# The lower halves of the gate one-hots made on ScalarE, two steps ahead, and ten row slots moved to the spreading units

## The chip, the cores and the metric

The kernel runs on one core of one Trainium2 chip. The metric is the device time of one execution in microseconds (us), lower is better. The engines are TensorE (PE in the rows, its weight loads PEld), VectorE (DVE), ScalarE (ACT), GpSimd (POOL) and SyncE (SP).

## What is computed

One layer of an encoder trunk over 1,024 tokens of width 1,024, in float32. The first half of the layer (gated mixing and a short convolution) is not touched by the change. The second half is PEER, a product-key mixture of 16,384 single-neuron experts:

```python
def block(xb):                       # 128 tokens
    q = (xb @ w_q).reshape(t, PEER_HEADS, 2, PEER_HALF)
    s = jnp.einsum('thpd,hpkd->thpk', q, sub_keys)
    s1, i1 = lax.top_k(s[:, :, 0], PEER_TOPK)
    s2, i2 = lax.top_k(s[:, :, 1], PEER_TOPK)
    ...
    top_s, sel = lax.top_k(cand_s, PEER_TOPK)
    idx = jnp.take_along_axis(cand_i, sel, axis=-1)
    gate = jax.nn.softmax(top_s, axis=-1)
    u = jnp.take(expert_u, idx, axis=0)
    act = jax.nn.gelu(jnp.einsum('thkd,td->thk', u, xb))
    v = jnp.take(expert_v, idx, axis=0)
    return jnp.einsum('thk,thkd->td', gate * act, v)
```

Each token has 8 heads times 16 chosen experts, 128 (expert, gate) pairs.

## The kernel before

The tokens are in two parts. Part A (3 blocks of 128 tokens) fetches only the experts that it chose: for each of 384 *slots* an indirect DMA on GpSimd's queue gathers one u row per token (128 rows of 4 KB), VectorE forms the dot product (`u_row`, L1016), and later a v row is gathered and added with its weight (`v_row`, L1025). Part B (5 blocks, 640 tokens) computes all 16,384 experts densely on TensorE: 64 units of kind E multiply the tokens by all expert u vectors and store the activations (`a_dram`), and 32 groups of two W units multiply coefficients by all expert v vectors. The coefficient is activation times gate, so the gates must be spread into a dense matrix (`g_dram`). That is done in 20 E units, numbers 40 to 59 (`E_SPREAD` = 40, `N_SPREAD` = 20), the *spreading units*. Everything runs concurrently; the row slots of part A are divided by hand among the units and groups of part B (`_sections`, L179 to L194): so many slots beside each unit.

Each expert table unit arrives as float32 in `stage`; ScalarE makes its upper float16 half (`make_hi`), VectorE the lower (`make_lo`, L913), and TensorE multiplies hi*hi, hi*lo and lo*hi (L1566 to L1568).

**The spreading.** A step q (8 in each spreading unit, 160 in all) covers 4 tokens. VectorE makes one-hots of both key halves, 1,024 float16 elements (`onehot_keys`, L1352), and multiplies the second key's one-hot by the upper and by the lower float16 half of the gates in one operation of 1,024 elements (`onehot_gate`, L1359, `oh_gate[:, q % 4, c]` with c = 0 for upper and 1 for lower). TensorE multiplies them in 8 matmuls of 128 columns into a psX bank (L1697), placed behind the third and the seventh of the eight chunks of each of the unit's four output tiles. ScalarE copies psX into `gbuf` (`spread_out`, L827). The one-hot buffers are a ring of 4 steps: `onehot_keys(q)` waits until TensorE has done step q - 4.

**ScalarE's order in a spreading unit** is, four times, two `spread_out` copies and the evacuation of one output tile; then, at the end of the unit, `make_hi` of the unit four ahead, the issue of the store to `g_dram` (L859), the issue of the store to `a_dram` (L863), and the small gelu on `dots`. An engine takes its instructions in order, so what is behind these DMA issues waits for them. All of ScalarE's activations stand on line L682 in the rows, a helper's line.

**The W groups.** For each group VectorE multiplies activations by gates (L1470), makes the lower half of the coefficients (L1479), makes two lower halves of weights (L913), adds three shared output tiles (L1490), and does its row slots. TensorE does 10 tiles of 12 matmuls of 512 columns.

`SLOTS` is 384. Slots not given to the units before are divided over 31 W groups: 194 of them before the change, so 6 in most groups and 7 in eight groups (numbers 3, 7, 11, 15, 19, 23, 27 and 30). The u rows run 24 slots (`LAG`) ahead of the v rows.

Of the kernel before, what the change touches and what calls it, by code (L numbers as in the profile page):

```python
# [178 lines left out]
def _sections():  # L179

    k = {("B", "U", u): 0 for u in (1, 2, 3)}
    for u in range(16):
        k["B", "M", u] = 3
    for u in range(4):
        k["B", "O", u] = 1
    for h in range(HEADS):
        k["B", "Q", h] = 2
    for e in range(2 * NGRP):
        k["B", "E", e] = 2 if e < E_SPREAD else 1 + e % 2 if e < E_SPREAD + N_SPREAD else 3
    groups = NGRP - 1  # L190
    left = SLOTS - sum(k.values())
    for g in range(groups):
        k["B", "W", 2 * g] = left * (g + 1) // groups - left * g // groups
    return k  # L194
# [65 lines left out]
def trunk_layer(nc, x, c_row, w_cond, b_col, w_front, ln_g, ln_b, w_spat, b_spat, conv_w,  # L260
                ln1_g, ln1_b, keys_t, u_units, v_units, u_rows, v_rows, ln2_g, ln2_b, out):
    with ExitStack() as ctx:
# [6 lines left out]
        def v3(ap, a):  # L269
            return ap.rearrange("p (a b) -> p a b", a=a)  # L270
# [115 lines left out]
        row_at += [R1[:, 1024 * i:1024 * (i + 1)] for i in range(5)]  # L386
        a_ring = v3(R1[:, :], 4)
        keys_t16 = v3(zone(15300, 640, F16), 2)
        gates16 = v3(zone(15940, 640, F16), 2)
        g_t = zone(16580, 640)  # L390
        iota_k4 = v3(zone(17220, 256, F16), P)
        gbuf = [zone(4096 * i, 4096).rearrange("p (k t) -> p k t", t=32) for i in range(2)]
        oh_keys = zone(8192, 4 * 512, F16).rearrange("p (r c k t) -> p r c k t", r=4, c=2, t=4)
        oh_gate = zone(10240, 4 * 512, F16).rearrange("p (r c k t) -> p r c k t", r=4, c=2, t=4)
# [80 lines left out]
        weight_ready = sem("weight_ready")  # L475
        oh_keys_ready = sem("oh_keys_ready")
        oh_ready = sem("oh_ready")
        prod_ready = sem("prod_ready")
        c_hi_ready = sem("c_hi_ready")
        c_ready = sem("c_ready")  # L480
# [11 lines left out]
        def wait_x(eng, a):  # L492
            eng.wait_ge(x_ready, a + 1)
# [186 lines left out]
        def _(act):  # L680
# [77 lines left out]
            for n, (x, kind, u) in enumerate(UNITS):  # L758
# [20 lines left out]
                elif kind == "U":  # L779
                    if u % 2 == 0:  # L780
                        act.wait_ge(evA_free, EVA[x] + 5 + u // 2)
                        feature(n, evAd[x], ACT.Gelu_apprx_tanh)
                    else:
                        act.wait_ge(evB_free, EVB[x] + 8 + u // 2)
                        feature(n, evB[x], ACT.Gelu_apprx_tanh)
                elif kind == "M":
                    q = u // 4
                    if u % 4 == 0:
                        act.wait_ge(evA_free, EVA[x] + 7 + q)
                        feature(n, evAd[x])  # L790
                    elif u % 4 == 2:
                        act.wait_ge(evC_free, EVC[x] + 4 + q)
                        feature(n, evC[x])
                    else:
                        act.wait_ge(evB_free, EVB[x] + 10 + 2 * q + u % 4 // 2)
                        feature(n, evB[x], ACT.Tanh, 0.5 * DESCALE)
                elif kind == "O" and x == "A":
                    for b in range(SB):
                        evacuate(t + b, xt[x][:, b, u * UC:(u + 1) * UC])
                elif kind == "O":  # L800
                    if u == 0:
                        for b in range(DB):
                            for c in range(4):
                                evacuate(T_O + 4 * b + c, xt[x][:, b, c * UC:(c + 1) * UC])
                            if b:
                                root(R_OB + 2 * (b - 1), slice(SB + b - 1, SB + b))
                                root(R_OB + 2 * (b - 1) + 1, slice(SB + b - 1, SB + b))

                            before = ("B", "O", b - 2) if b >= 2 else ("B", "M", 15)
                            if b != 1:  # L810
                                gelu_dots(SEC_OF[before])
                        root(R_OB + 2 * (DB - 1), slice(NB - 1, NB))
                        root(R_OB + 2 * (DB - 1) + 1, slice(NB - 1, NB))
                        gelu_dots(SEC_OF["B", "O", 3])
                        h_hi_tiles("H2B", 0, 2 * KD)
                elif kind == "Q":
                    if x == "A" and u == 0:
                        act.wait_ge(x1_stored["A"], 16)
                        act.wait_ge(h2_ready, 1)
                    feature(n, rk[x]["qb"][u % 2])  # L820
                elif kind == "E":
                    wait(act, a_stored[u % 4], 16 * (u // 4))
                    if u == 0:
                        act.wait_ge(x1_stored["B"], 16 * DB)
                    slot = v3(a_ring[:, u % 4, :], 2)

                    def spread_out(r):  # L827
                        i = u - E_SPREAD
                        for q in range(2):
                            at = 2 * r + q  # L830
                            a = X_G + 8 * i + at
                            wait_x(act, a)
                            activation(gbuf[i % 2][:, :, 4 * at:4 * at + 4],
                                       psX[a % 4][:, :].rearrange("p (t k) -> p k t", t=4),
                                       ACT.Copy, 1.0 / GS).then_inc(x_free[a % 4], 1)

                    spreading = E_SPREAD <= u < E_SPREAD + N_SPREAD
                    if spreading and u >= E_SPREAD + 2:
                        act.wait_ge(g_stored[u % 2], 16 * ((u - E_SPREAD) // 2))
                    for j in range(2):  # L840
                        for half in range(2):
                            if spreading:
                                spread_out(2 * j + half)
                            evacuate(t + 2 * j + half, slot[:, j, half * HB:(half + 1) * HB], ACT.Gelu_apprx_tanh)
# [52 lines left out]
        def _(dve):  # L897
# [429 lines left out]
            def idx_t():  # L1327
# [10 lines left out]
                for i in range(4):  # L1338
                    a = X_IDX + 5 - i
                    dve.wait_ge(x_free[a % 4], a // 4 + 1)  # L1340
                step(V.tensor_copy(gates16[:, 0, :], g_t))
                settle()
                step(V.tensor_tensor(gates16[:, 1, :], g_t, gates16[:, 0, :], ALU.subtract))
                step(V.tensor_copy(iota_k4, iota_i[:, :].unsqueeze(2).to_broadcast([P, P, 4])))
                settle()

# [7 lines left out]

            def onehot_gate(q):
                dve.wait_ge(oh_keys_ready, q + 1)
                at = gates16[:, :, 4 * q:4 * q + 4].unsqueeze(2).to_broadcast([P, 2, P, 4])
                both = oh_keys[:, q % 4, 1:2, :, :].to_broadcast([P, 2, P, 4])
                V.tensor_tensor(oh_gate[:, q % 4, :, :, :], both, at, ALU.mult).then_inc(oh_ready, 1)  # L1359

            def spreads(unit):

# [193 lines left out]
        def _(pe):  # L1556
# [87 lines left out]
            for n, (x, kind, u) in enumerate(UNITS):  # L1644
# [43 lines left out]
                elif kind == "E" and E_SPREAD <= u < E_SPREAD + N_SPREAD:  # L1688
                    def spread(r, s):
                        if s not in (2, 6):  # L1690
                            return
                        q = 8 * (u - E_SPREAD) + 2 * r + (s == 6)
                        pe.wait_ge(oh_ready, q + 1)
                        ps = x_tile(X_G + q)
                        for t in range(4):
                            for c in range(2):
# [92 lines left out]
```

## Time and profile before

| | |
|---|---|
| time, median of 3 runs | 3223.4 us (3216.7 to 3224.55) |
| the profiled execution | 3218.67 us, of which the span of its instructions 3216.9 us |
| mean granted TensorE clock | 0.962 of full |
| TensorE busy | 2928.1 us, 91% of the span |
| VectorE busy | 2635.7 us, 82% |
| ScalarE busy | 812.4 us, 25% |
| GpSimd busy | 1013.3 us, 31% |
| DMA traffic | 917.49 MB, mean 285 GB/s |

Busy time counts instructions that compute; the issue of a DMA isn't counted, although the engine that issues it can stand still for it. The shares are averages over stages of very different kinds, so they don't tell which engine sets the pace in the stage that is changed.

### The profile page before, as it was taken

Reading aid. Unit: us, or ns where it says so; the run is one execution under the profiler, and the core shown is the slowest. Engines: PE = TensorE matmul, PEld = TensorE weight load, DVE = VectorE, ACT = ScalarE, POOL = GpSimd, SP = SyncE. Lnnn points to the kernel's source line nnn. Section 1 sums busy time; section 2 is a strip of 40 time slices with the busy share of each in tenths; the row PEclk is TensorE's granted clock in tenths of the full one; section 3 lists DMA queues with packets and bytes.
Section 4 is the critical chain, followed back from the end, with each engine's and each line's share of the span. In section 5 each row is a group of like instructions: output and inputs, shape, how many; then the busy total and the mean of one; then the engine's idle time right before and its main releaser. Section 6 shows DMA issues by size and latency. Waiting matters only on the chain.

```text
span 3216.9 us, 46792 instructions
## 1 busy us (share of the span) xinstructions
PE 2928.1 (91%) x19088; PEld 1916.7 (60%) x19088; DVE 2635.7 (82%) x4587; ACT 812.4 (25%) x1191; POOL 1013.3 (31%) x778
## 2 busy tenths in 40 slices
PE   4899979997898679999999899999799999999994
PEld 3556666665676556777777688887444444444442
DVE  6865557996765869999999777777699999999987
ACT  2333322111111322222222233333222222222220
POOL 0000000003553104344434311112366666666630
PEclk9999989998999889999999999999899999999997
DMA  9888534333898247877777788888999999999973
GB/s 357 310 321 321 192 142 158 119 112 145 318 358 304 85 178 251 297 276 277 278 283 264 263 262 262 262 262 280 364 392 414 414 414 414 411 415 413 413 285 124
DMA packets 266230, 917.49 MB, mean 285 GB/s; under 512 B 20464, under 2 KB 102432, under 8 KB 222752
## 3 DMA queue, kind: packets, MB, share of 16 engines
q1 hardware_dynamic: 63968, 427.91, 34.7%
q0 software_dynamic: 110592, 402.70, 33.2%
q10 hardware_dynamic: 91456, 83.89, 8.0%
q8 instruction: 151, 2.47, 0.3%
q14 instruction: 63, 0.52, 0.0%
HBM read 771.79 MB, written 142.63 MB: 284 GB/s over the span
## 4 chain that ended last, share of the span: by engine, by line
PE 59%; DVE 25%; issue 9%; DMA 6%; ACT 1%; SPq 0%; POOL 0%; DVEq 0%
PE psU L1566 17%; PE psU L1568 17%; PE psU L1567 17%; PE psX L1697 5%; DVE acc_sp L1025 3%; DMA R<-in_v_rows,idx_sp 2%; DVE w L913 2%; DVE Z L1470 2%; DVE rows L1016 2%; DVE R L1016 2%; DVE Z L1490 1%; PE psX L1566 1%; PE psX L1567 1%; PE psX L1568 1%; DMA rows<-in_v_rows,idx_sp 1%
## 5 line engine op out<-in xcount | busy, mean ns | idle before, releaser
L1566 PE MATMUL psU<-hB,w 128*128 128x320 f16 x3072 | 924.4, 301 | 31.8 <-ACT R L682 19.8
L1568 PE MATMUL psU<-hB,w 128*128 128x320 f16 x3072 | 921.0, 300 | 0.9 <-issue 0.9
L1567 PE MATMUL psU<-hB,w 128*128 128x320 f16 x3072 | 921.1, 300 | 0.0
L913 DVE SCALAR_TENSOR_TENSOR w<-stage,w 128x2048 f16<-128x2048 f32 x176 | 402.6, 2288 | 172.8 <-ACT w L682 168.5
L682 ACT ACTIVATE w<-stage 128x2048 f16<-128x2048 f32 x176 | 335.4, 1906 | 359.9 <-PE psX L1568 294.9
L675 POOL DMA_INDIRECT rows<-in_v_rows,idx_sp x214 | 284.2, 1328 | 349.4 <-DVE rows L1016 210.2
L1566 PEld LDWEIGHTS psU<-hB,w 128*128 128x128 f16 x3072 | 304.1, 99 | 145.6 <-issue 33.5
L675 POOL DMA_INDIRECT rows<-in_u_rows,idx_sp x204 | 253.9, 1245 | 430.5 <-DVE rows L1016 372.3
L1568 PEld LDWEIGHTS psU<-hB,w 128*128 128x128 f16 x3072 | 301.0, 98 | 119.0 <-issue 0.5
L1567 PEld LDWEIGHTS psU<-hB,w 128*128 128x128 f16 x3072 | 304.1, 99 | 112.9 <-issue 1.1
L1566 PE MATMUL psX<-w,Z 128*128 128x512 f16 x768 | 296.0, 385 | 48.2 <-DVE Z L1490 33.0
L1566 PE MATMUL psU<-w,Z 128*128 128x512 f16 (+1 forms) x768 | 267.1, 348 | 44.3 <-DVE Z L1479 22.3
L1567 PE MATMUL psX<-w,Z 128*128 128x512 f16 x768 | 295.7, 385 | 0.0
L1568 PE MATMUL psX<-w,Z 128*128 128x512 f16 x768 | 295.3, 384 | 0.0
L1025 DVE SCALAR_TENSOR_TENSOR acc_sp<-rows,weight_sp,acc_sp 128x1024 f32<-128x1024 f32 x214 | 269.2, 1286 | 14.8 <-DMA rows<-in_v_rows,idx_sp 8.4
L1567 PE MATMUL psU<-w,Z 128*128 128x512 f16 (+1 forms) x768 | 267.0, 348 | 0.0
L1568 PE MATMUL psU<-w,Z 128*128 128x512 f16 (+1 forms) x768 | 266.7, 347 | 0.0
L1016 DVE SCALAR_TENSOR_TENSOR rows<-rows,h_sp 128x1024 f32<-128x1024 f32 x204 | 243.6, 1218 | 5.3 <-DMA rows<-in_u_rows,idx_sp 3.0
L682 ACT ACTIVATE Z<-psU 128x320 f32<-128x320 f32 (+1 forms) x224 | 99.5, 451 | 551.0 <-PE psU L1568 426.0
L675 POOL DMA_INDIRECT R<-in_v_rows,idx_sp x108 | 174.3, 1614 | 137.3 <-DVE R L1016 87.2
L682 ACT ACTIVATE R<-psU 128x320 f32<-128x320 f32 (+1 forms) x296 | 123.1, 427 | 368.8 <-PE psU L1568 332.1
L1566 PE MATMUL psU<-Z,w 128*128 128x384 f16 (+1 forms) x640 | 206.5, 323 | 2.9 <-ACT Z L682 2.9
(237 smaller groups left out, 4627.8 us busy)
## 6 DMA issues: line engine op xcount, KB each, us to landing
stage<-in_u_units SPq DMA_DIRECT2D x64, 1024.0 KB
stage<-in_v_units SPq DMA_DIRECT2D x64, 1024.0 KB
stage<-in_w_front SPq DMA_DIRECT2D x48, 1024.0 KB
hl_dram<-w SPq DMA_DIRECT2D x48, 1024.0 KB, 5.5
w<-hl_dram SPq DMA_DIRECT2D x48, 1024.0 KB
a_dram<-R ACTq DMA_DIRECT2D x64, 640.0 KB
g_dram<-Z ACTq DMA_DIRECT2D x20, 2048.0 KB, 15.4
Z<-a_dram SPq DMA_DIRECT2D x32, 1280.0 KB, 12.1
```

What stands on the lines that cost most here:

```text
L675: pool.indirect_dma_start(row_at[r], None, u_rows if table == "u" else v_rows, bass.IndirectOffsetOnAxis(ap=idx_sp[:, slot:slot + 1], axis ...
L682: return nc.scalar.activation(dst, src, func, scale=scale)
L913: V.scalar_tensor_tensor(w[:, n % NW, 1, :], stage[:, v % 2, :], WS, w[:, n % NW, 0, :], ALU.mult, ALU.subtract).then_inc(lo_done, 1)
L1016: V.scalar_tensor_tensor(row_at[r], row_at[r], 1.0, h2_sp[:, slot % SB, :], ALU.mult, ALU.mult, accum_out=dots[:, c % 4, j:j + 1]).then_in ...
L1025: V.scalar_tensor_tensor(dst, row_at[r], weight_sp[:, slot:slot + 1], dst, ALU.mult, ALU.add).then_inc(row_used, 1)
L1470: ins = V.scalar_tensor_tensor(a, a, AS, G_t[g % 2][:, :, j, :], ALU.mult, ALU.mult)
L1490: V.tensor_tensor(dst, ps_shared[:, :], dst, ALU.add).then_inc(v_free, 1)
L1566: mm(ps, lhs[0](k), rhs[0](k), start=start and s == 0, stop=False)
L1567: mm(ps, lhs[0](k), rhs[1](k), start=False, stop=False)
L1568: last = mm(ps, lhs[1](k), rhs[0](k), start=False, stop=stop and s == n - 1)
L1697: ins = mm(ps[:, t * P:(t + 1) * P], oh_keys[:, q % 4, 0, :, t], oh_gate[:, q % 4, c, :, t], start=(c == 0), stop=(c == 1))
```

## The change

```diff
@@ _sections
-        k["B", "E", e] = 2 if e < E_SPREAD else 1 + e % 2 if e < E_SPREAD + N_SPREAD else 3
+        k["B", "E", e] = 2 if e < E_SPREAD + N_SPREAD else 3
@@ buffers
-        gates16 = v3(zone(15940, 640, F16), 2)
+        gates16 = zone(15940, 320, F16)
...
+        gate_lo = zone(17476, 640)
@@ scalar, kind E
+                    def gates_lo(q):
+
+                        if q >= 8 * N_SPREAD:
+                            return
+                        act.wait_ge(oh_keys_ready, q + 1)
+                        for i in range(4):
+                            ins = activation(oh_gate[:, q % 4, 1, :, i], oh_keys[:, q % 4, 1, :, i], ACT.Copy,
+                                             gate_lo[:, 4 * q + i:4 * q + i + 1])
+                        ins.then_inc(oh_lo_ready, 1)
+
                     def spread_out(r):
                         i = u - E_SPREAD
                         for q in range(2):
                             at = 2 * r + q
                             a = X_G + 8 * i + at
+                            gates_lo(8 * i + at + 2)
                             wait_x(act, a)
...
+                    if u == E_SPREAD:
+                        gates_lo(0)
+                        gates_lo(1)
@@ vector, onehot_gate
-                at = gates16[:, :, 4 * q:4 * q + 4].unsqueeze(2).to_broadcast([P, 2, P, 4])
-                both = oh_keys[:, q % 4, 1:2, :, :].to_broadcast([P, 2, P, 4])
-                V.tensor_tensor(oh_gate[:, q % 4, :, :, :], both, at, ALU.mult).then_inc(oh_ready, 1)
+                at = gates16[:, 4 * q:4 * q + 4].unsqueeze(1).to_broadcast([P, P, 4])
+                key = oh_keys[:, q % 4, 1, :, :]
+                V.tensor_tensor(oh_gate[:, q % 4, 0, :, :], key, at, ALU.mult).then_inc(oh_ready, 1)
@@ tensor, spread
                         pe.wait_ge(oh_ready, q + 1)
+                        pe.wait_ge(oh_lo_ready, q + 1)
```

VectorE's `onehot_gate` now makes the upper half alone (512 elements). The lower half of step q is made by four ScalarE activations of 128 elements, one for each token, whose scale is a column of `gate_lo` in SBUF; they stand just ahead of the copy of step q - 2. The lower gates stay in float32. TensorE waits for both halves. The twenty spreading units had 1 or 2 row slots in turn (30 in all) and now have 2 each (40), so the W groups have 184 slots in place of 194: 6 in each but groups 0 and 15, which have 5.

On ScalarE, at the boundary from the first spreading unit to the second, before the change. Z<-psX is a `spread_out` copy, R<-psU the evacuation of an output tile, w<-stage `make_hi`, and dots the gelu of the row section:

```order
L682 ACTIVATE R<-psU 128x320 [waits tile_ready]
L682 ACTIVATE w<-stage 128x2048 [waits stage_in0]
L859 DMA g_dram<-Z 128x32x128 [waits x_free1,x_free2,x_free0,x_free3]
L863 DMA a_dram<-R 128x1280 [waits tile_free]
L682 ACTIVATE dots<-dots 128x2 [waits row_used]
L682 ACTIVATE Z<-psX 128x128x4 [waits x_ready,a_stored1]
L682 ACTIVATE Z<-psX 128x128x4 [waits x_ready]
```

The same place after the change, with Z<-Z 128x128 the new activations:

```order
L684 ACTIVATE R<-psU 128x320 [waits tile_ready]
L684 ACTIVATE w<-stage 128x2048 [waits stage_in0]
L875 DMA g_dram<-Z 128x32x128 [waits x_free1,x_free2,x_free0,x_free3]
L879 DMA a_dram<-R 128x1280 [waits tile_free]
L684 ACTIVATE dots<-dots 128x2 [waits row_used]
L684 ACTIVATE Z<-Z 128x128 [waits oh_keys_ready,a_stored1]
L684 ACTIVATE Z<-Z 128x128 x3
L684 ACTIVATE Z<-psX 128x128x4 [waits x_ready]
L684 ACTIVATE Z<-Z 128x128 [waits oh_keys_ready]
L684 ACTIVATE Z<-Z 128x128 x3
L684 ACTIVATE Z<-psX 128x128x4 [waits x_ready]
```

The first four new activations behind the two stores belong to step 2 of the unit that begins there; those of its steps 0 and 1 stand ahead of the stores, in the unit before.

On TensorE, at the end of a spreading unit's work between two steps of the spreading, before and then after:

```order
L1566 MATMUL psU<-hB,w 128x320
L1567 MATMUL psU<-hB,w 128x320
L1568 MATMUL psU<-hB,w 128x320
L1697 MATMUL psX<-Z 128x128 [waits x_free2,oh_ready]
L1697 MATMUL psX<-Z 128x128 x7
```

```order
L1582 MATMUL psU<-hB,w 128x320
L1583 MATMUL psU<-hB,w 128x320
L1584 MATMUL psU<-hB,w 128x320
L1714 MATMUL psX<-Z 128x128 [waits x_free2,oh_lo_ready,oh_ready]
L1714 MATMUL psX<-Z 128x128 x7
```

Nothing moves on TensorE, but each step has one wait more, `oh_lo_ready`, and all that is queued behind it waits too.

## Rows read from the trace of the kernel before

**Rows 1.** Section 4 of the page: shares of the chain that ended last.

```profile
PE 59%; DVE 25%; issue 9%; DMA 6%; ACT 1%; SPq 0%; POOL 0%; DVEq 0%
```

**Rows 2.** Windows: us, busy time of each engine, TensorE clock, DMA share, GB/s.

```profile
1820.60:2230.60 410.00, 410.00 (x3192) 337.28 (x3190) 322.89 (x442) 154.61 (x278) 70.03 (x61) 1.00 0.81 262
2305.60:3070.00 764.40, 741.01 (x3369) 331.51 (x3370) 744.88 (x822) 171.84 (x111) 473.23 (x343) 0.98 1.02 411
3070.00:3160.00 90.00, 89.00 (x413) 40.14 (x411) 63.49 (x60) 16.53 (x11) 16.96 (x13) 1.00 0.65 254
```

**Rows 3.** Timeline of ScalarE at a unit boundary: start, duration, instruction, idle before.

```profile
1983.87 0.60 ACT L682 ACTIVATE Z<-psX 128x512 f32<-128x512 f32 x1 [1.98 <-PE psX L1697]
1984.36 0.43 ACT L682 ACTIVATE R<-psU 128x320 f32<-128x320 f32 x1
1984.57 0.38 ACTq L859 DMA_DIRECT2D g_dram<-Z  x1
1984.68 1.92 ACT L682 ACTIVATE w<-stage 128x2048 f16<-128x2048 f32 x1
1984.99 5.38 ACTq L863 DMA_DIRECT2D a_dram<-R  x1
1990.42 0.20 ACT L682 ACTIVATE dots<-dots 128x1 f32<-128x1 f32 x1 [3.83 <-issue]
1990.53 1.08 ACT L682 ACTIVATE Z<-psX 128x512 f32<-128x512 f32 x2
```

**Rows 4.** Timeline of TensorE's weight loads: step 2 of the same unit.

```profile
1990.30 0.70 PEld L1697 LDWEIGHTS psX<-Z 128*128 128x128 f16 x6
```

**Rows 5.** Groups by line of ScalarE, 1840:2231: busy us, mean ns, idle before.

```profile
L682 ACT ACTIVATE Z<-psX 128x512 f32<-128x512 f32 x153 | 89.7, 599 | 168.9 <-PE psX L1697 165.5 <-issue 3.5
L682 ACT ACTIVATE R<-psU 128x320 f32<-128x320 f32 x76 | 33.1, 435 | 0.0
L682 ACT ACTIVATE dots<-dots 128x2 f32<-128x2 f32 x10 | 2.0, 204 | 39.5 <-issue 39.5
L682 ACT ACTIVATE dots<-dots 128x1 f32<-128x1 f32 x9 | 1.8, 203 | 36.4 <-issue 36.4
```

**Rows 6.** Groups by line of VectorE, 1840:2231.

```profile
L1352 DVE TENSOR_TENSOR Z<-Z 128x1024 f16<-128x1024 f16 x149 | 102.7, 689 | 66.9 <-PE psX L1697 64.4
L1359 DVE TENSOR_TENSOR Z<-Z 128x1024 f16<-128x1024 f16 x149 | 102.7, 689 | 2.9
```

**Rows 7.** Timelines of TensorE and ScalarE at the first spreading unit.

```profile
1820.58 0.94 PEld L1697 LDWEIGHTS psX<-Z 128*128 128x128 f16 x8
1821.83 0.19 ACT L682 ACTIVATE dots<-dots 128x2 f32<-128x2 f32 x1
```

**Rows 8.** Timeline of VectorE: lower coefficients, once in each W group.

```profile
2321.60 2.81 DVE L1479 TENSOR_TENSOR Z<-Z 128x2560 f16<-128x2560 f32 x1
...
2484.90 2.81 DVE L1479 TENSOR_TENSOR Z<-Z 128x2560 f16<-128x2560 f32 x1
...
2511.69 2.81 DVE L1479 TENSOR_TENSOR Z<-Z 128x2560 f16<-128x2560 f32 x1
...
2540.68 2.81 DVE L1479 TENSOR_TENSOR Z<-Z 128x2560 f16<-128x2560 f32 x1
...
2567.18 2.81 DVE L1479 TENSOR_TENSOR Z<-Z 128x2560 f16<-128x2560 f32 x1
...
3081.95 2.81 DVE L1479 TENSOR_TENSOR Z<-Z 128x2560 f16<-128x2560 f32 x1
```

**Rows 9.** Timeline of TensorE in the W groups, behind a short and a long wait.

```profile
2397.22 0.38 PE L1566 MATMUL psX<-w,Z 128*128 128x512 f16 x1 [1.16 <-DVE Z L1490]
...
2398.95 0.38 PE L1568 MATMUL psX<-w,Z 128*128 128x512 f16 x1
...
2426.28 0.59 PE L1566 MATMUL psX<-w,Z 128*128 128x512 f16 x1 [3.00 <-issue]
...
2429.65 0.38 PE L1568 MATMUL psX<-w,Z 128*128 128x512 f16 x1
```

More of the change, by code:

```diff
@@ L477, in trunk_layer @@
         oh_ready = sem("oh_ready")
+        oh_lo_ready = sem("oh_lo_ready")
         prod_ready = sem("prod_ready")
@@ L1340, in idx_t @@
                     dve.wait_ge(x_free[a % 4], a // 4 + 1)
-                step(V.tensor_copy(gates16[:, 0, :], g_t))
+                step(V.tensor_copy(gates16, g_t))
                 settle()
-                step(V.tensor_tensor(gates16[:, 1, :], g_t, gates16[:, 0, :], ALU.subtract))
+                step(V.tensor_tensor(gate_lo, g_t, gates16, ALU.subtract))
                 step(V.tensor_copy(iota_k4, iota_i[:, :].unsqueeze(2).to_broadcast([P, P, 4])))
```

## The prediction

> **What bounds the kernel now.** I read the chain that ended last first: 59% of the span is TensorE and 25% VectorE [rows 1], so the pace changes hands between stages, and each stage must be read by itself. The windows do that [rows 2]. In the 20 spreading units (1820.6 to 2230.6 us) TensorE is busy for all of the 410 us at full clock; a unit takes 410 / 20 = 20.5 us, a step of the spreading 2.57 us. VectorE has 87 us to spare there and ScalarE seems to have 255. In the W groups (2305.6 to 3070) VectorE is busy for 745 of 764 us and TensorE waits 23. DMA is at 1.02 of its engines and 411 GB/s, so it is about as full as VectorE. In the last three groups no u rows are left and TensorE is busy for 89 of 90 us.
>
> So VectorE time taken out of the spreading units is worth nothing where it is taken, since VectorE already waits for TensorE there [rows 6]. It pays only through the ten slots that leave the W groups. Against that stands whatever the new work on ScalarE makes TensorE wait.
>
> **ScalarE at a unit boundary.** Its 155 busy us of 410 mislead. The timeline of one boundary [rows 3] shows why: after the last evacuation (1984.36) the issue of the g_dram store takes 0.38 us, but the a_dram store behind it holds ScalarE's queue for 5.38 us, to 1990.37. The gelu behind it begins at 1990.42 after 3.83 us of idling, and the first two copies of the new unit begin at 1990.53, late. Before the change this is harmless: TensorE's four psX banks cover it. TensorE's step 2 of that unit begins at 1990.30 [rows 4], when ScalarE is not yet free.
>
> After the change the four activations for step 2 stand behind these two stores and the gelu. Those for steps 0 and 1 stand ahead and are in time, and from step 3 on ScalarE gains on TensorE. So TensorE must wait once at each boundary, at step 2.
>
> **The price of one wait.** Four activations of 128 elements: on these rows a copy of 512 takes 599 ns and one of 1 or 2 takes 203 to 204 [rows 5], so 128 take about 204 + 126 x (599 - 204) / 510 = 302 ns. Back to back the gelu and the copy behind it start 0.11 us apart with 0.20 us of duration [rows 3], an overlap of 0.09. Lower bound for four: 0.30 + 3 x 0.21 = 0.93 us. Without overlap: 4 x 0.30 = 1.20 us. No row shows an activation whose scale is a column of SBUF or which writes each fourth element, so I take 1.20, the dearer of the two. A bound from far above is four at the price of a copy of 512, 2.4 us.
>
> The boundary shown is one of the shorter: the idling ahead of the gelu is (39.5 + 36.4) / 19 = 3.99 us in the mean [rows 5], 0.16 more. The halves are ready at 1990.53 + 0.16 + 1.20 = 1991.89, against 1990.30: a wait of 1.59 us. Since the block on ScalarE begins with the evacuation of the unit's last tile, it moves along with TensorE, so nothing is won back. There are 19 boundaries between spreading units: 19 x 1.59 = 30.2 us (25.1 with the lower bound).
>
> The first unit adds one. TensorE begins step 0 at 1820.58 [rows 7], but ScalarE has `make_hi` and the gelu first and can begin the halves only at 1821.83 + 0.11. Ready 1.20 later, at 1823.14: 2.6 us. Together the spreading units lose about 33 us (27 to 33 between the two readings).
>
> The Trainium skill (ScalarE: Activation LUTs, What ACT_TABLE_LOAD costs) gives 186 ns + 0.833 ns per element for an activation with immediate scale, about 93 ns more for each pointer operand, and an overlap of about 93 ns. That agrees with the 599, 204 and 0.09 above; no row here shows the pointer operand. By it four would take an estimated 0.386 + 3 x 0.293 = 1.27 us, and the units would lose 34 us, not 33.
>
> **Is ScalarE fast enough for the rest?** In a unit it has the block (about 6.3 us from the last evacuation on), 8 copies, 3 evacuations, and now 32 activations. The copies come 0.5 us apart, (1.08 - 0.60) [rows 3], and the evacuations about 0.36. That is 6.3 + 4.0 + 1.1 = 11.4 us, and with 32 x 0.30 = 9.6 it is 21.0, under the 20.5 + 1.6 = 22.1 us of the lengthened unit. It fits, with 0.03 us for each activation to spare.
>
> **VectorE in the spreading units.** The upper half alone is between half of 689 ns and all of it, 0 to 0.34 us saved in each of 160 steps; the ten slots add rows. Odd units have two slots with the dear one-hots already, and TensorE doesn't wait in them. The cost is nothing, covered by the waits for TensorE (67 us in 19 units [rows 6]). If that cover were gone it would be ten slots times about 2.5 us. The ten slots are also 20 gathers more on GpSimd's queue and 10.5 MB more DMA, at a DMA share of 0.81 [rows 2]: room enough. The additional wait on TensorE costs nothing where it is already met, since the step begins without a gap behind its matmuls now, with two waits.
>
> **The W groups.** From `coefficients_lo` to the next, the interval with six slots takes 2511.69 - 2484.90 = 26.8 or 2567.18 - 2540.68 = 26.5 us, the one with seven 2540.68 - 2511.69 = 29.0 [rows 8]. So a slot is worth 2.55 us here. DMA alone would give a like number: two gathers of 0.524 MB at 411 GB/s [rows 2] are 2.55 us, so it doesn't matter which of the two is the limit. The 28 intervals from 2321.60 to 3081.95 take 27.2 us in the mean. Seven of the eight seven-slot groups and both of the new five-slot groups lie in them, nine slots: 9 x 2.55 = 23 us. The tenth (group 30) lies where TensorE sets the pace. TensorE's floor is 120 matmuls; eight of them take 2398.95 - 2397.22 = 1.73 us [rows 9], so 25.9 us for a group. The five-slot group 15 would want 24.0, which loses up to 1 us of the gain. I take 22 us, between 18 and 27: some intervals hold short waits of VectorE for late rows which may stay or go.
>
> **A rule that speaks against the change.** VectorE makes both halves in 689 ns [rows 6] and has 87 us to spare in this stage [rows 2]; by the price above ScalarE needs 1.2 us for one. Left there, the slots alone would give 3223.4 - 22 = 3201. The Trainium skill (ScalarE: Activation LUTs, Rules for kernel authors) says to use VectorE, not ScalarE, for a multiplication; the trace agrees. It changes nothing in the sum below, which counts ScalarE's price.
>
> **The sum** against the profiled execution of 3218.67 us: + 33 - 22 = + 11, so about 3230. The median of the runs is 4.7 us above that execution, so the number to compare with it is 3223.4 + 10 = 3233, rounded down a little since the lower price of the activations would make it + 5. What a measurement of this kernel can tell is about 0.3%, 9.7 us, and the forecast lies on that line.
>
> **Rivals.**
>
> *The price is low or W gives more (within 0.3%).* With 0.93 us for four, 27 - 22 = + 5; with W at 27 as well, 0. Overlap of neighbouring activations speaks for it; the column of scales speaks against it.
>
> *Faster.* The queue behind the a_dram store frees early. The 5.38 us stand only where a g_dram store is ahead; at the first unit, without one, the gelu follows `make_hi` at once [rows 7]. If the wait for the queue shrank to under 4 us, as other traffic or a later issue may make it, the halves for step 2 would be in time; only the first 2.6 us would stay, and the time would be 3223.4 + 3 - 22 = 3204. Against it: 19 boundaries idle for 4 us in the mean, and nothing in the change touches the two stores. It decides for faster once the loss in the spreading units is under 12 us, 0.5 us a boundary. That is less than ScalarE's own lateness (0.39) plus one activation (0.30).
>
> *ScalarE becomes the bound.* Over 0.33 us for each activation every 0.1 us adds 3.2 us to a unit. At 0.39 it would be 11.4 + 12.5 = 23.9 us in place of 22.1, 36 us more in all: 3269. Nothing in the rows asks for it, but the room is thin.
>
> *The clock falls at each wait.* A wait of 3.00 us is followed by matmuls of 0.59 us, eight of them in 2429.65 - 2426.28 = 3.37 us where they take 1.73 at full clock: 1.6 us lost. After 1.16 us there is no such loss [rows 9]. A wait of 1.6 lies between. At all 19 boundaries it would be + 30, so 3263.
>
> **Chances.** The main case, a wait of 1.2 to 1.8 us at each boundary and 18 to 27 us back in W, has 0.74 and its own range is 3219 to 3242; 0.37 of it falls within 0.3% and 0.37 above. ScalarE as the bound 0.08, the clock 0.06: both slower. The freed queue and a W gain beyond the main range together 0.12, faster. So faster 0.12, same 0.37, slower 0.51. For 8 in 10 the range leaves out most of the faster case and the far end of the slower ones: 3215 to 3260.
>
> **What would show it.** In the profile after: TensorE idle at step 2 of units 41 to 59 and nowhere else there, 1.2 to 1.8 us each, ended by ScalarE's new activations; the spreading units 437 to 444 us long; the store to a_dram still holding ScalarE for over 5 us; VectorE's upper-half operation well under 0.69 us; all intervals of W at 26.5 but one or two, and the 28 of them some 22 us shorter. The forecast fails if the first of these is absent, if the new activations take over 0.35 us each, or if W's intervals stay at 27.2.

## The result and the profile after

The changed kernel takes 3254.0 us in the median of four runs (3249.1 to 3263.2), the kernel before, on the same chip, 3220.8 (3216.7 to 3224.6): a ratio of 1.0108, 95% interval 1.0094 to 1.0122. It is slower by about 33 us, where the forecast was 10. The profiled executions stand at 3250.8 us against 3218.67, + 32.1; the accounts below are made against this pair.

The chain that ended last, in the profile after; TensorE had 59% and VectorE 25% [rows 1]:

```profile
PE 53%; DVE 29%; issue 9%; DMA 6%; ACT 2%; SPq 0%; POOL 0%; ACTq 0%; DVEq 0%
```

The windows of the same three stages (us, busy time of PE, PEld, DVE, ACT, POOL, granted clock, DMA share, GB/s):

```profile
1825.00:2284.80 459.80, 423.97 (x3195) 340.59 (x3196) 301.11 (x468) 357.09 (x914) 73.79 (x78) 0.97 0.78 253
2358.80:3090.00 731.20, 719.19 (x3312) 323.10 (x3313) 712.40 (x786) 168.39 (x109) 453.08 (x322) 1.00 1.02 411
3090.00:3180.00 90.00, 90.00 (x419) 40.82 (x418) 66.10 (x57) 19.82 (x11) 22.09 (x14) 1.00 0.68 261
```

Against [rows 2] the spreading stage is 460 us long in place of 410. TensorE does about the same number of matmuls in it (3,195 against 3,192) but now stands idle for 36 us, and the clock is 0.97 where it was 1.00. TensorE's weight loads mark the stage's ends and two of the late steps 2 between:

```profile
1825.05 0.84 PEld L1714 LDWEIGHTS psX<-Z 128*128 128x128 f16 x8 [3.68 <-issue]
...
1970.18 0.85 PEld L1714 LDWEIGHTS psX<-Z 128*128 128x128 f16 x8 [4.25 <-issue]
...
1993.47 0.84 PEld L1714 LDWEIGHTS psX<-Z 128*128 128x128 f16 x8 [1.84 <-DVE Z L1375]
...
2282.79 0.94 PEld L1714 LDWEIGHTS psX<-Z 128*128 128x128 f16 x8
```

The stage begins 4.5 us later than before (1820.58 [rows 7]), and its last step is 53.3 us later (2229.47 before). The row at 1993.47 names VectorE's half as the releaser, but VectorE had finished that half at 1983.80. Who came last is seen on ScalarE, at the boundary of [rows 3]:

```profile
1985.22 0.60 ACT L684 ACTIVATE Z<-psX 128x512 f32<-128x512 f32 x1 [0.60 <-PE psX L1714]
1985.71 0.43 ACT L684 ACTIVATE R<-psU 128x320 f32<-128x320 f32 x1
1985.92 0.38 ACTq L875 DMA_DIRECT2D g_dram<-Z  x1
1986.03 1.91 ACT L684 ACTIVATE w<-stage 128x2048 f16<-128x2048 f32 x1
1986.34 5.43 ACTq L879 DMA_DIRECT2D a_dram<-R  x1
1991.81 0.20 ACT L684 ACTIVATE dots<-dots 128x2 f32<-128x2 f32 x1 [3.87 <-issue]
1991.92 1.48 ACT L684 ACTIVATE Z<-Z 128x128 f16<-128x128 f16 x4
1993.15 0.68 ACT L684 ACTIVATE Z<-psX 128x512 f32<-128x512 f32 x1
1993.73 1.47 ACT L684 ACTIVATE Z<-Z 128x128 f16<-128x128 f16 x4
```

The a_dram store holds ScalarE's queue for 5.43 us (5.38 before), the gelu comes behind it, and the four halves of step 2 end at 1993.40. TensorE's step 2 begins at 1993.47. At each of the 19 boundaries step 2 begins 0.07 us behind the end of these four. The groups of ScalarE and VectorE, 1850:2284, give the new operations' prices:

```profile
L684 ACT ACTIVATE Z<-Z 128x128 f16<-128x128 f16 x600 | 221.4, 565 | 0.0
L684 ACT ACTIVATE Z<-psX 128x512 f32<-128x512 f32 x151 | 99.4, 658 | 17.3 <-PE psX L1714 17.2
L1368 DVE TENSOR_TENSOR Z<-Z 128x1024 f16<-128x1024 f16 x148 | 102.2, 690 | 128.0 <-PE psX L1714 125.5 <-issue 2.5
L1375 DVE TENSOR_TENSOR Z<-Z 128x512 f16<-128x512 f16 x148 | 62.5, 422 | 2.5
```

One activation alone is 565 ns long, but they overlap: four last 1.48 us, so they start 0.305 us apart. ScalarE, which waited 165 us for TensorE's matmuls before [rows 5], waits 17 now. VectorE's idling went from 67 us [rows 6] to 128.

**Waits of two lengths.** At 17 of the 19 boundaries TensorE's weight loads wait 1.77 to 2.19 us at step 2, 32.0 us together (the idle of the rows less the 0.04 us that lie between any two loads). At the other two they wait 4.22 and 4.62. (Its matmuls, whose modelled ends come later, idle 0.3 us less each time, hence the 36 us of the window. The prediction and this account go by the weight loads.) There the store held the queue longer, as ScalarE's rows ahead of the step 2 at 1970.18 show:

```profile
1960.64 7.84 ACTq L879 DMA_DIRECT2D a_dram<-R  x1
1968.53 0.20 ACT L684 ACTIVATE dots<-dots 128x2 f32<-128x2 f32 x1 [6.28 <-issue]
```

One thing sets these two apart from the other 17 holds. The DMA queues of the profile show, 5.4 us behind the issue of the g_dram store, the start of a 16 KB packet of the kind instruction, while the hold goes on. Of the others one has such a packet start within it, 0.9 us behind that issue, and is 5.52 us long.

**Half clock.** Behind 7 of the 19 waits the matmuls run at half speed for some 3 us. TensorE's timeline behind one of them:

```profile
1876.18 1.10 PE L1714 MATMUL psX<-Z 128*128 128x128 f16 x8 [1.63 <-DVE Z L1375]
...
1877.94 0.47 PE L1584 MATMUL psU<-hB,w 128*128 128x320 f16 x1
1878.20 0.47 PE L1582 MATMUL psU<-hB,w 128*128 128x320 f16 x1
...
1881.30 0.30 PE L1582 MATMUL psU<-hB,w 128*128 128x320 f16 x1
1881.44 0.30 PE L1583 MATMUL psU<-hB,w 128*128 128x320 f16 x1
```

A matmul of 320 columns starts 0.26 us behind the one before at 1878, 0.14 at 1881. The window over these 3 us gives the granted clock, 0.50 of full (the value ahead of the DMA share):

```profile
1877.70:1880.70 3.00, 3.00 (x17) 2.08 (x16) 0.73 (x2) 3.00 (x10) 0.00 (x0) 0.50 1.05 409
```

By how late the steps behind these waits come, that costs 6.8 us over the stage. The first unit has such a stretch too, behind its wait at step 0.

**W.** The marks of [rows 8], first and last of the 28 intervals:

```profile
2374.30 2.81 DVE L1495 TENSOR_TENSOR Z<-Z 128x2560 f16<-128x2560 f32 x1
...
3114.30 2.81 DVE L1495 TENSOR_TENSOR Z<-Z 128x2560 f16<-128x2560 f32 x1
```

That is 740.0 us where it was 3081.95 - 2321.60 = 760.35, a gain of 20.35 us.

| term | forecast | measured in the profiled execution |
|---|---|---|
| waits at step 2, 19 boundaries | + 30.2 | + 32.0 + 8.8 = + 40.8 |
| first unit | + 2.6 | + 4.5 until its step 0 (0.8 of it from before the stage), 1.1 behind it (half clock) |
| half clock at the boundaries | 0 | + 6.8 |
| W, 28 intervals | - 22 | - 20.35 |
| sum | + 11 | + 32.9 (all of the kernel: + 32.1) |

### The profile page after: what moved, and what is told of

The parts are those of the page before. It is cut to its first block, busy times and chain, and to the rows that moved or that the text cites. A ratio compares the mean times of both kernels' runs of the same rounds, so it can differ in the third digit from the quotient of the medians.

```text
span 3249.0 us, 47429 instructions
## 1 busy us (share of the span) xinstructions
PE 2934.5 (90%) x19088; PEld 1917.9 (59%) x19088; DVE 2591.8 (80%) x4586; ACT 1016.8 (31%) x1830; POOL 1016.6 (31%) x778
## 4 chain that ended last, share of the span: by engine, by line
PE 53%; DVE 29%; issue 9%; DMA 6%; ACT 2%; SPq 0%; POOL 0%; ACTq 0%; DVEq 0%
PE psU L1582 15%; PE psU L1583 15%; PE psU L1584 15%; DVE w L929 4%; PE psX L1714 4%; DVE acc_sp L1041 4%; DMA R<-in_v_rows,idx_sp 2%; DVE R L1032 2%; DVE Z L1486 2%; DVE rows L1032 2%; DVE Z L1506 1%; ACT w L684 1%; DVE Z L1495 1%; DVE Z L1368 1%; DVE acc_sp L1259 1%
## 5 line engine op out<-in xcount | busy, mean ns | idle before, releaser
L684 ACT ACTIVATE Z<-Z 128x128 f16<-128x128 f16 (+2 forms) x689 | 319.5, 647 | 385.6 <-DVE Z L1486 346.8
L677 POOL DMA_INDIRECT rows<-in_u_rows,idx_sp x212 | 267.4, 1261 | 425.0 <-DVE rows L1032 229.6
L677 POOL DMA_INDIRECT rows<-in_v_rows,idx_sp x210 | 270.7, 1289 | 358.4 <-DVE rows L1032 298.2
L1582 PE MATMUL psX<-w,Z 128*128 128x512 f16 x768 | 291.7, 380 | 36.6 <-DVE Z L1506 35.1
L1583 PE MATMUL psX<-w,Z 128*128 128x512 f16 x768 | 291.7, 380 | 0.0
L1584 PE MATMUL psX<-w,Z 128*128 128x512 f16 x768 | 291.6, 380 | 0.0
L1032 DVE SCALAR_TENSOR_TENSOR rows<-rows,h_sp 128x1024 f32<-128x1024 f32 x212 | 253.1, 1219 | 4.1 <-DMA rows<-in_u_rows,idx_sp 2.9
L1368 DVE TENSOR_TENSOR Z<-Z 128x1024 f16<-128x1024 f16 x160 | 110.4, 690 | 136.3 <-PE psX L1714 133.8
```

The source lines that it names most:

```text
L677: pool.indirect_dma_start(row_at[r], None, u_rows if table == "u" else v_rows, bass.IndirectOffsetOnAxis(ap=idx_sp[:, slot:slot + 1], axis ...
L684: return nc.scalar.activation(dst, src, func, scale=scale)
L1032: V.scalar_tensor_tensor(row_at[r], row_at[r], 1.0, h2_sp[:, slot % SB, :], ALU.mult, ALU.mult, accum_out=dots[:, c % 4, j:j + 1]).then_in ...
L1368: V.tensor_tensor(oh_keys[:, q % 4, :, :, :], iota_k4.unsqueeze(1).to_broadcast([P, 2, P, 4]), at, ALU.is_equal).then_inc(oh_keys_ready, 1)
L1582: mm(ps, lhs[0](k), rhs[0](k), start=start and s == 0, stop=False)
L1583: mm(ps, lhs[0](k), rhs[1](k), start=False, stop=False)
```

## Experiments

The theory at the start: the halves of step 2 are late because they stand behind the a_dram store in ScalarE's queue. Rivals: ScalarE's work for a unit is too long, or something in the ten moved slots does it.

**The two parts apart.** e1 is the kernel before with the new slots alone, e2 the changed kernel with the old slots.

```diff
e1: @@ _sections of the kernel before
-        k["B", "E", e] = 2 if e < E_SPREAD else 1 + e % 2 if e < E_SPREAD + N_SPREAD else 3
+        k["B", "E", e] = 2 if e < E_SPREAD + N_SPREAD else 3
e2: @@ _sections of the changed kernel
-        k["B", "E", e] = 2 if e < E_SPREAD + N_SPREAD else 3
+        k["B", "E", e] = 2 if e < E_SPREAD else 1 + e % 2 if e < E_SPREAD + N_SPREAD else 3
```

> The slots alone are moved (2 in each spreading unit, 184 left for the W groups); both halves of the gate one-hots stay on VectorE. Theory: the W groups give back 20 us as they did with the full change, and the spreading units keep their 410 us, since VectorE has room for two slots in each unit even with both halves: 3221 - 20 = 3201 us. Rival: two slots in each unit need VectorE's relief; then TensorE waits in the spreading units for VectorE's one-hots and the gain is under 10 us.

> ScalarE makes the lower halves as in the change, but the row slots stay as before (1 and 2 in turn, 194 in W). Theory: the whole loss of the spreading units, 53 us, and none of the gain: 3221 + 53 = 3274 us, with W as before. Rival: part of the 53 us is from the rows that were moved (more gathers beside the stores); then it is clearly under 3265 us.

e1 took 3199.8 us against 3221.1 (ratio 0.9932, 0.9915 to 0.9948), with no wait of TensorE in the spreading stage. e2 took 3272.8 (1.0155, 1.0135 to 1.0174). So the slots give 21 us, the halves cost 52, and - 21 + 52 is near the 33 measured. e2 has store holds of 7.86, 7.68 and 8.37 us at three boundaries, so the long ones don't come from the ten slots.

**The halves three steps ahead, and the two stores swapped.**

```diff
e3: @@ scalar, spread_out
-                            gates_lo(8 * i + at + 2)
+                            gates_lo(8 * i + at + 3)
... (and gates_lo(2) behind gates_lo(1) at the start)
e4: @@ scalar, end of a unit: the a_dram store is issued ahead of the g_dram store
+                    act.wait_ge(tile_free, t + 4)
+                    act.dma_start(a_dram[u // 2, :, 2 * (u % 2):2 * (u % 2) + 2, :], v3(a_ring[:, u % 4, :], 2)
+                                  ).then_inc(a_stored[u % 4], 16)
...
-                    act.wait_ge(tile_free, t + 4)
-                    act.dma_start(a_dram[u // 2, :, 2 * (u % 2):2 * (u % 2) + 2, :], v3(a_ring[:, u % 4, :], 2)
-                                  ).then_inc(a_stored[u % 4], 16)
```

> The full change, but each lower half is made three steps ahead in place of two, so that those of steps 0, 1 and 2 of a unit stand ahead of the two stores. The same 640 activations. Theory (order: step 2's half stands behind the store that holds ScalarE's queue): the wait at step 2 of 19 boundaries goes, and with it the half clock behind it; about 4 us at the first unit stay, so 3221 + 4 - 20 = 3205 us. Rival (ScalarE has simply too much work for a unit): the work is the same, and the time stays near 3254 us.

> The full change, with the issue of the a_dram store put ahead of the g_dram store at the end of a unit. Theory (the a_dram store is held because the g_dram store ahead of it fills the queue): a_dram issues in 0.33 us, g_dram in about 0.4, ScalarE's hold of 5.4 us goes, the wait at step 2 too, about 3205 us. Rival (any second store at the end of a unit is held): the hold moves to the g_dram store and the time stays near 3254 us.

e4: 3202.6 us (0.994, 0.9923 to 0.9957). ScalarE at the same boundary:

```profile
1988.57 0.33 ACTq L872 DMA_DIRECT2D a_dram<-R  x1
1989.06 0.38 ACTq L878 DMA_DIRECT2D g_dram<-Z  x1
1990.22 0.20 ACT L684 ACTIVATE dots<-dots 128x2 f32<-128x2 f32 x1
1990.32 1.49 ACT L684 ACTIVATE Z<-Z 128x128 f16<-128x128 f16 x4
```

Issued first, the a_dram store costs 0.33 us, and nothing waits. TensorE waits at no boundary, only at the first unit. The same halves, at the same price, cost 52 us with the stores in one order and about 3 (3202.6 - 3199.8) in the other. That settles the place of the loss.

e3 missed: 3247.9 us (1.0081, 1.0065 to 1.0098) where 3205 was expected. Step 2 waits no more, but step 3 does, 1.1 to 4.8 us at 11 boundaries and up to 0.5 at the other 8. One of the longest, on ScalarE and on TensorE's weight loads:

```profile
2027.61 0.38 ACTq L876 DMA_DIRECT2D g_dram<-Z  x1
2027.72 1.89 ACT L684 ACTIVATE w<-stage 128x2048 f16<-128x2048 f32 x1
2028.03 9.01 ACTq L880 DMA_DIRECT2D a_dram<-R  x1
```

```profile
2038.73 0.85 PEld L1715 LDWEIGHTS psX<-Z 128*128 128x128 f16 x8 [4.71 <-issue]
```

Two questions came of it: why the hold is 9 us in place of 5.4, and whether a normal hold would do. On GpSimd's queue a gather is issued at about the same time:

```profile
2027.14 0.94 POOL L677 DMA_INDIRECT Z<-in_v_rows,idx_sp  x1 [4.21 <-DVE Z L1033]
```

At 15 of e3's 19 boundaries a gather is issued between 0.5 us ahead of the g_dram store's issue and 1.1 us behind it, and the holds there are 5.5 to 9.1 us (mean 7.3). At the other four they are 5.4 to 6.1. Within the five longest, 8.1 to 9.1 us, a packet of the kind instruction starts too.

**The price of the activations.** e5 takes the column of scales away (a constant 0.0 in its place, so the lower halves are left out of the result). e6 puts four activations of 32 elements into a spare zone ahead of the halves of each step 2.

```diff
e5: @@ scalar, gates_lo
-                            ins = activation(oh_gate[:, q % 4, 1, :, i], oh_keys[:, q % 4, 1, :, i], ACT.Copy,
-                                             gate_lo[:, 4 * q + i:4 * q + i + 1])
+                            ins = activation(oh_gate[:, q % 4, 1, :, i], oh_keys[:, q % 4, 1, :, i], ACT.Copy, 0.0)
e6: @@ scalar, gates_lo, ahead of the four
+                        if q % 8 == 2:
+                            for i in range(4):
+                                activation(spare[:, 32 * i:32 * i + 32], oh_keys[:, q % 4, 1, 0:32, i], ACT.Copy,
+                                           gate_lo[:, 4 * q + i:4 * q + i + 1])
```

> The full change with a constant scale of 0 in place of the column of gate_lo in the 640 new activations, so the lower halves are left out of the result. Theory: the four activations then cost what I put into the sum (first 0.30 us, then 0.21 each, 0.93 us in all, in place of the measured 1.48), the wait at step 2 falls by 0.5 us to 1.3 to 1.4, and fewer boundaries are followed by half clock; about 19 x 0.5 + 6 = 15 us faster than the change, near 3237 us. Rival: the activations of 128 elements cost 0.305 us each whatever their scale is; then nothing changes and it stays near 3252.

> The full change, with four more activations of 32 elements (to a place nobody reads) ahead of the halves of step 2 of each unit. Theory: the wait at step 2 grows by their 0.9 us to 2.8, and half clock follows at nearly all 19 boundaries, 1.2 to 1.6 us each, in place of half of them: 19 x 0.9 + 10 x 1.3 = 30 us slower than the change, near 3282. Rival (the half clock has nothing to do with the length of the wait): the waits add 17 us and the number of boundaries with half clock stays at 9, near 3269.

e5 missed: 3247.5 us in a single run, not 3237. That is 32.9 us above the kernel before on the same chip (3214.6), as the changed kernel's 33.2. ScalarE's timeline at a boundary:

```profile
1986.08 1.35 ACT L684 ACTIVATE Z<-Z 128x128 f16<-128x128 f16 x4
1987.16 0.68 ACT L684 ACTIVATE Z<-psX 128x512 f32<-128x512 f32 x1
```

Four take 1.35 us against 1.48, so they start 0.267 us apart in the mean in place of 0.305. The column of scales costs 0.04 us each; the rest of the price is in the activation itself. The two long waits grew (4.9 and 5.0 us), and half clock followed 7 of the 19 as before, so the whole gained nothing that a single run can tell. e6 took 3277.8 us in a single run (before: 3214.6). The waits at step 2 grew to 2.61 to 2.85 (four longer still), and half clock followed 15 of the 19, not 7.

**No row slots in the spreading units.** Their 40 go to the W groups, which lengthens those and isn't of interest here. e7 does it with the halves three steps ahead, e10 with them two ahead.

```diff
-        k["B", "E", e] = 2 if e < E_SPREAD + N_SPREAD else 3
+        k["B", "E", e] = 2 if e < E_SPREAD else 0 if e < E_SPREAD + N_SPREAD else 3
... (and, in VectorE's part of a spreading unit)
-                        if q % 2:
+                        if q % 2 and SECTION[unit]:
                             next(rest, None)
```

> The kernel with the halves three steps ahead, but with no row slots in the spreading units (224 are left for the W groups, which makes those slower by some 95 us; only the spreading units are to be compared). Theory (the hold of the a_dram store grows from 5.4 to 6 to 9 us when a gather is issued on GpSimd's queue around the issue of the g_dram store, as it is at 16 of 20 boundaries three steps ahead): all holds are 5.4 to 5.9 us and TensorE waits nowhere but in the first unit. Rival (the longer holds come from something else, the earlier work of ScalarE for one): holds of 7 to 9 us stay at a third or more of the boundaries.

> The full change's activations, two steps ahead, but with no row slots and so no gathers in the spreading units (224 slots left for W; only the spreading units are to be compared). If the gathers make the long holds of 7.8 and 8.2 us, all holds are 5.3 to 5.9 here, the wait at step 2 is 1.9 us at every boundary and the two of over 4 us are gone; the number of boundaries with half clock stays near 7. If the long holds come from something else, two or three boundaries with a wait of over 4 us stay.

Without gathers each of the some 40 holds in the two kernels is 5.30 to 5.90 us; not one is long. Yet e7's step 3 still waits, 0.9 to 1.5 us at 17 boundaries (1.0 mostly). ScalarE in it, from the last two steps of a unit into the next:

```profile
2007.63 0.41 ACT L684 ACTIVATE R<-psU 128x320 f32<-128x320 f32 x1
2007.94 1.47 ACT L684 ACTIVATE Z<-Z 128x128 f16<-128x128 f16 x4
2009.15 0.67 ACT L684 ACTIVATE Z<-psX 128x512 f32<-128x512 f32 x1
2009.73 1.48 ACT L684 ACTIVATE Z<-Z 128x128 f16<-128x128 f16 x4
2010.94 0.69 ACT L684 ACTIVATE Z<-psX 128x512 f32<-128x512 f32 x1
2011.54 0.41 ACT L684 ACTIVATE R<-psU 128x320 f32<-128x320 f32 x1
2011.74 0.38 ACTq L876 DMA_DIRECT2D g_dram<-Z  x1
...
2012.16 5.60 ACTq L880 DMA_DIRECT2D a_dram<-R  x1
2017.88 1.48 ACT L684 ACTIVATE Z<-Z 128x128 f16<-128x128 f16 x4 [4.13 <-DVE Z L1369]
```

Outside of the hold ScalarE doesn't idle at all. Its unit is 6.3 us from the last evacuation to the first halves behind the store, 8 x 1.21 from halves to copy, 8 x 0.58 from copy to what follows, and 3 x 0.31 for the other evacuations: 21.6 us. The units come 21.5 us apart, where TensorE needs 20.5. Three steps ahead, ScalarE sets the pace, even with short holds.

e10's waits are 1.66 to 2.10 us (mean 1.79), none over 4, and its clock is halved behind 3 of 19, where about 7 were expected. The two long waits aside, the changed kernel has 5 of 17, and the difference to 3 of 19 is too small to tell anything. That the length of a wait alone doesn't decide on the clock is seen within the changed kernel: it is halved behind a wait of 1.90 us (unit 42) and stays full behind one of 2.18 (unit 50).

**A version that is faster.** With the stores swapped there is room for more slots in the spreading units. e8 has e4's order, 50 slots (2 and 3 in turn), and issues the halves of steps 0 and 1 at the end of unit 39, just ahead of the spreading. e9 is the kernel before with 50 slots, e11 that with the stores swapped too, and e12 is e8 again, beside e11 on one chip.

```diff
-        k["B", "E", e] = 2 if e < E_SPREAD + N_SPREAD else 3
+        k["B", "E", e] = 2 if e < E_SPREAD else 2 + e % 2 if e < E_SPREAD + N_SPREAD else 3
... (e9 and e11: the same new line in the kernel before; e8, e11 and e12: the stores as in e4)
... (e8, e12)
-                    if u == E_SPREAD:
-                        gates_lo(0)
-                        gates_lo(1)
...
+                if (x, kind, u) == ("B", "E", E_SPREAD - 1):
+                    gates_lo(0)
+                    gates_lo(1)
```

> A version meant to be faster than all: halves on ScalarE, a_dram store ahead of the g_dram store, the halves of steps 0 and 1 made before the last unit ahead of the spreading ends its work on ScalarE, and 50 slots in the spreading units (2 and 3 in turn), 174 left for W. Theory: no wait at the boundaries, 1 to 2 us at the first unit, and the W groups go from VectorE's 26.5 us towards TensorE's 25.9, at most 28 x 0.6 = 17 us: 3202 - 3 - 14 = 3185 us. Rival: three slots are too much beside the one-hots, TensorE waits in every other unit, 3195 or more.

> Both halves on VectorE as before the change, and 50 slots in the spreading units (2 and 3 in turn). It shows what ScalarE's part is worth once more slots are moved. A unit with three slots asks VectorE for 8 x 1.32 + 6 x 1.2 + 2.2 + 0.2 = 20.2 us of TensorE's 20.6, one with two for 17.8, so on the mean there is room. Theory: TensorE waits little (under 5 us) and the W groups gain as much as with ScalarE's halves: about 3187 us. Rival: the units with three slots are too tight in their order, TensorE waits a us or more in each of ten, 3197 or more.

> Both halves on VectorE, 50 slots in the spreading units, and the a_dram store ahead of the g_dram store. The two waits of 1 to 1.5 us that the long holds (10.5 and 11.0 us) gave without the swap go: 2 to 3 us faster than without it, ratio to the kernel before near 0.989. Rival: the units with three slots are late on VectorE by themselves, and it stays at 0.990.

> The version with the halves on ScalarE, the swapped stores and 50 slots once more, beside the one with both halves on VectorE on the same chip: it tells what ScalarE's halves are worth once the stores are swapped. Both run the W groups at TensorE's pace and neither waits at the boundaries, so they should agree within 0.1%, with 1 us at the first unit for or against.

| kernel | median, us | ratio to before |
|---|---|---|
| e8: ScalarE's halves, swapped, 50 slots | 3178.4 | 0.9888 (0.9868 to 0.9907) |
| e9: VectorE's halves, not swapped, 50 slots | 3188.4 | 0.9898 (0.9879 to 0.9918) |
| e11: VectorE's halves, swapped, 50 slots | 3178.4 | 0.9880 (0.9863 to 0.9896) |
| e12: as e8 | 3181.9 | 0.9886 (0.9870 to 0.9903) |

The windows of the spreading stage, of e11 and then of e12:

```profile
1818.55:2228.70 410.15, 410.15 (x3191) 337.82 (x3189) 364.90 (x502) 156.41 (x278) 120.96 (x100) 1.00 0.93 313
```

```profile
1819.80:2229.80 410.00, 409.97 (x3188) 337.65 (x3189) 322.44 (x498) 366.84 (x914) 112.57 (x100) 1.00 0.93 311
```

TensorE is busy throughout in both, and VectorE has 45 us to spare even with both halves and 50 slots. So the move of the halves to ScalarE is worth nothing that these runs can tell, with no store in its way either. The gain comes with the slots: 21 us for ten in e1. e9 and e11 ran on different chips and the intervals of their ratios overlap, so what the swap adds to e9 isn't settled; the swap without other changes wasn't run. e8 came out 7 us under its forecast on a chip where the kernel before was 6 us faster too. e11, without the new activations, is 1.2% under the kernel before, and by the two ratios 2.3% under the changed one.

In e9 ScalarE's queue shows longer holds still, three of 9.2 to 11.0 us. Two of them reach TensorE, which waits 0.96 and 1.45 us at step 4; in e11 nothing waits. Three of ScalarE's rows at one of them:

```profile
1862.80 0.38 ACTq L859 DMA_DIRECT2D g_dram<-Z  x1
1863.21 10.52 ACTq L863 DMA_DIRECT2D a_dram<-R  x1
1873.79 0.20 ACT L682 ACTIVATE dots<-dots 128x2 f32<-128x2 f32 x1 [8.96 <-issue]
```

## Why the prediction was right in kind and short in size

**The place was right, and shown.** The forecast put the loss at step 2 of units 41 to 59, behind the a_dram store, and nowhere else but the first unit. The profile has it there, the store's hold is over 5 us, and e4 takes it away by moving the store alone. But the 33 us lie beyond the main case. Its range ended at 3242 and its waits at 1.8 us, where most are longer. The time is inside the wide range only because that left room for the rival of the clock and for ScalarE as the bound; the clock came true in part, and the longer holds, which no rival had, fell into the same room by luck. Of the signs, the spreading stage was to be 437 to 444 us long and was some 463 with the first unit's wait, and the activations, 0.37 us each if four are divided up, were past the limit of 0.35 set for them.

No term alone carries the miss of 22 us (32.9 in the table against 10.8): half clock 7.9 with the first unit's, the price of the activations 5.5, the long holds 5.1, the first unit's wait 1.9, W 1.7.

**The term that was mis-sized at every boundary is the price of one wait**, four activations at 4 x 0.30 = 1.20 us. They take 1.48 us. Put into the prediction's formula, 1.59 - 1.20 + 1.48 = 1.87 us, and 17 boundaries measure 1.88. That is 5.5 us of the 22. The spacing of the starts was right, 0.305 us against the 0.30 taken; what was short is the length of a single one, 565 ns against 302, which stands once at the end of the four. The line drawn between 2 and 512 elements didn't hold for this form: half precision, SBUF to SBUF, each fourth element. e5 shows that the scale from SBUF is little of it (538 ns without it). The Trainium skill (ScalarE: Activation LUTs, What ACT_TABLE_LOAD costs) puts a pointer operand at about 93 ns. The spacing here changed by 38 ns, and the measurement decides. The estimate made from that page for four, 1.27 us, was short too.

**The hold was taken as constant.** Two boundaries had 7.84 and 8.24 us, which adds 5.1 us to the 19 waits (8.8 - 2 x 1.88). The prediction had a rival for a shorter hold and none for a longer one. Gathers have to do with it: there are none of these holds without gathers (e7, e10), eight of over 7 us in e3 and the longest in e9, whose gathers come nearer to the stores. How a gather lengthens the hold isn't shown. In the changed kernel the gathers stand at the same distance at the two long holds as at the short ones. What goes along with the length there is the instruction packet in the midst of the hold. It isn't enough by itself: in e10, without gathers, holds with such a packet 5.3 and 5.5 us behind the g_dram issue are 5.62 and 5.76 us long, and in e9, with gathers, two are 6.23 and 5.65. Nor is it always there: none starts within e2's hold of 7.68. A long hold also has more time to meet one. So the cause stays open.

**The clock** was the rival with 0.06, "at all 19 boundaries". It came true at 7, for 6.8 us, and once more in the first unit. The sum had it at nothing. Its premise that a wait of 1.6 "lies between" was right; the case that it comes true in part was missing. e6 gives 15 of 19 at waits of 2.6 us and more, e10 3 of 19 at 1.79 in the mean, and e7 none of 17 at 0.9 to 1.5.

**The first unit** was sized at 2.6 us and cost 3.6 until its step 0 (4.47 less 0.83) and 1.1 of half clock behind it. The four at 1.48 us are 0.3 of the difference. The rest is that ScalarE's last evacuation ahead of the spreading began at 1821.29, 1.60 us later than before where the whole kernel was 0.83 later; why isn't shown.

**"It fits, with 0.03 us for each activation to spare"** held only because of the wait itself. ScalarE's unit is 21.6 us, not 21.0 (the copies stand 0.58 us apart from what follows and not 0.5), against 20.5 of TensorE and 22.4 with the wait. The rival in which ScalarE becomes the bound isn't what the changed kernel shows, but it is what stops the obvious repair, as e3 and e7 showed.

**W** gave 20.35 us for the 22 taken. TensorE's floor is part of that: its long waits there are gone (719 of 731 us busy at clock 1.00). Most intervals of six slots are 26.2 to 26.6 us, six are 27.2 to 27.8. The number 22 was near, but not slot by slot: of the nine slots counted at 2.55 us, the one of group 0 gave 0.2 us (26.07 to 25.90) and that of group 27 nothing (23.64 to 23.59); shorter waits elsewhere made up for part of it. **VectorE's** side held: the upper half fell to 422 ns, nobody waits for the ten slots, and that saving is worth nothing in this stage. The rule weighed against the change, leave both halves on VectorE, was right: its 3201 is e1's 3200.

## What to carry to other kernels

Before work is put onto an engine that looks idle, read one whole period of its timeline with the DMA issues in it. An issue that holds the queue is not busy time, yet all that is put behind it is late by it; the cheapest repair may be the order of two issues. And move work off an engine only in a stage where someone waits for that engine: here the gain lay in the slots, and it was to be had without the new operations.

## What the hardware showed that wasn't expected

- The same a_dram store holds ScalarE's queue 0.33 us when issued ahead of the g_dram store, 5.3 to 11.0 us when issued right behind it. The g_dram store itself is issued in 0.38 us, and in 0.38 to 1.85 with the a_dram store ahead (e4). What the issue waits for in that time the records don't show.
- An activation of 128 half-precision elements, each fourth in source and destination, is 565 ns long and starts 0.305 us behind the one before; one of 2 float32 elements is 203 ns long.
- Half clock (1.2 GHz, granted clock 0.50) of some 3 us followed waits of 0.9 to 1.5 us in none of 17 cases (e7), waits of 1.6 to 2.2 us (a few longer) in 3 to 7 of 19, and waits of 2.6 us and more in 15 of 19 (e6). In this range its cost belongs in a forecast as a share.
